# Two projections of the first network with three groups side by side, and weighted values between two input tiles

## The reference

```
g = sigmoid(gate_logit).reshape(b, s, 3, d)
merged = (g[:, :, 0] * (y_fox @ w_o_fox[l])
          + g[:, :, 1] * (y_mla @ w_o_mla[l])
          + g[:, :, 2] * (y_sb @ w_o_sb[l]))
x = x + gt_a * (merged @ w_out[l])
u = rms_norm(x, g_ffn[l]) * (1 + sc_f) + sh_f
```

## Time and profile before

| what | value |
|---|---|
| median of 3 runs | 2102.11 us (2101.72 to 2104.12) |
| the profiled execution | 2101.66 us, its span 2099.9 us |
| TensorE busy | 2025.5 us (96%) |
| VectorE busy | 1624.7 us (77%) |
| ScalarE busy | 1171.1 us (56%) |
| mean granted TensorE clock | 0.992 |
| end of the attention, layer 0 | 264 to 306 us of the span |
| end of the attention, layer 1 | 738 to 779 us of the span |

### The profile page before, as it was taken

One profiled execution on the slowest core, in us unless ns is written; L12 is line 12 of the kernel. 1 busy time (PEld: TensorE's weight loads), 2 busy tenths in 40 slices (PEclk: granted clock), 3 DMA queues, 4 the chain that ended last, 5 costly groups with the idle time before them and its releaser, 6 DMA issues.

```text
span 2099.9 us, 37052 instructions
## 1 busy us (share of the span) xinstructions
PE 2025.5 (96%) x13975; PEld 1837.7 (88%) x13975; DVE 1624.7 (77%) x2668; ACT 1171.1 (56%) x2116; POOL 148.3 (7%) x233
## 2 busy tenths in 40 slices
PE   6999989999999989999999999999999999999998
PEld 6988989999988989998876888888888888899997
DVE  7788879966688879979787789786989426658983
ACT  6757746645557756646636555352544227646762
POOL 0100000000000000004000300001102000000000
PEclk9999999999999999999999999999999999999999
DMA  9766547865766547876341334546634222244553
GB/s 367 272 216 203 189 146 258 282 229 167 241 216 210 180 153 258 300 243 219 126 162 62 107 131 156 194 141 240 211 130 142 99 90 101 81 161 141 184 178 110
DMA packets 106624, 383.03 MB, mean 182 GB/s; under 512 B 11504, under 2 KB 16128, under 8 KB 105184
## 3 DMA queue, kind: packets, MB, share of 16 engines
q1 hardware_dynamic: 77584, 280.21, 39.2%
q0 software_dynamic: 25792, 94.31, 13.4%
q10 hardware_dynamic: 3088, 6.29, 0.8%
HBM read 379.71 MB, written 1.05 MB: 181 GB/s over the span
## 4 chain that ended last, share of the span: by engine, by line
PE 77%; DVE 12%; ACT 4%; issue 4%; DMA 3%; POOL 0%; POOLq 0%; SPq 0%; DVEq 0%; ACTq 0%
PE ps L1099 19%; PE ps L1102 18%; PE ps L1103 18%; DVE ring_l L2379 3%; PE ps L1120 3%; PE ps L1124 3%; PE ps L1125 3%; DVE ada_junk L2402 2%; DMA work<-adas_in 2%; PE ps L1142 2%; ACT ring_r L1722 2%; PE ps L1145 1%; PE ps L1146 1%; PE ps L1672 1%; DMA ring<-tape_in 1%
## 5 line engine op out<-in xcount | busy, mean ns | idle before, releaser
L1099 PE MATMUL ps<-part,ring_l 128*128 128x256 f32 (+1 forms) x3445 | 1038.6, 301 | 13.7 <-DVE ring_l L2379 7.3
L1103 PE MATMUL ps<-part,ring_r 128*128 128x256 f32 (+1 forms) x3445 | 1027.2, 298 | 0.0
L1102 PE MATMUL ps<-part,ring_r 128*128 128x256 f32 (+1 forms) x3445 | 1026.1, 298 | 0.0
L2379 DVE TENSOR_TENSOR ring_l<-ring,ring_r 128x1024 fp32r<-128x1024 f32 x514 | 626.4, 1232 | 149.5 <-ACT ring_r L1722 146.8
L1722 ACT ACTIVATE ring_r<-ring 128x1024 fp32r<-128x1024 f32 x514 | 533.8, 1056 | 356.8 <-DMA ring<-tape_in 259.1
L1099 PEld LDWEIGHTS ps<-part,ring_l 128*128 128x128 f32 x3445 | 652.0, 189 | 44.2 <-DVE part L2379 7.7
L1103 PEld LDWEIGHTS ps<-part,ring_r 128*128 128x128 f32 x3445 | 648.6, 188 | 24.7
L1102 PEld LDWEIGHTS ps<-part,ring_r 128*128 128x128 f32 x3445 | 648.5, 188 | 24.3
L2402 DVE SCALAR_TENSOR_TENSOR ada_junk<-work 128x1024 bf16<-128x1024 f32 x272 | 334.0, 1228 | 50.2 <-DMA work<-adas_in 38.2
L1142 PE MATMUL ps<-part,ring_l 128*128 128x256 f32 (+1 forms) x400 | 125.5, 314 | 20.9 <-DVE part L2379 11.1
L1146 PE MATMUL ps<-part,ring_r 128*128 128x256 f32 (+1 forms) x400 | 121.5, 304 | 0.0
(11 more groups left out here) (287 smaller groups left out, 2109.0 us busy)
## 6 DMA issues: line engine op xcount, KB each, us to landing
ring<-tape_in SPq DMA_DIRECT2D x514, 512.0 KB, 3.4
work<-adas_in POOLq DMA_DIRECT2D x176, 512.0 KB, 4.7
work<-ada_first_in SPq DMA_DIRECT2D x8, 1024.0 KB, 17.5
work<-bias_in ACTq DMA_DIRECT2D x1, 2048.0 KB, 7.9
x<-x_t_in SPq DMA_DIRECT2D x1, 1024.0 KB, 7.5
work<-cond_in POOLq DMA_DIRECT2D x1, 1024.0 KB, 8.9
x<-ctx_in ACTq DMA_DIRECT2D x1, 1024.0 KB, 13.1
x<-dist_in ACTq DMA_DIRECT2D x1, 1024.0 KB, 6.2
```

The lines of the kernel that those rows point to most:

```text
L1099: mm = pe.matmul(dst, lhsT=wl, rhs=mr, start=(k == 0), stop=False)
L1102: pe.matmul(dst, lhsT=wr, rhs=mr, start=False, stop=False)
L1103: mm = pe.matmul(dst, lhsT=wr, rhs=ml, start=False, stop=(k == len(moving) - 1))
L2379: return dve.tensor_tensor(dst, whole, rounded_part.bitcast(F32), ALU.subtract)
```

## The change

- The third branch's first three groups run side by side (input tile by input tile, with a wait for each y), and pv11 is issued inside them, behind input tile 1 (`VALUES_LATE`). Before, pv11 stood ahead of the branch. The other five groups run one after the other as before.
- w_out's first three groups run side by side; the others as before.
- The host reorders the tape's tiles to match.
- ScalarE rounds by hand where `READ` no longer has a name: `round_behind` after the last mix tile, and one panel more behind each of the first three squares.
- VectorE's `ahead` for w_out0, 1 and 2 uses leads of 6, 7 and 8, since the three groups now start in the same panel.

```diff
+VALUES_LATE = 1
...
     for b, n in enumerate(("w_o_fox", "w_o_mla", "w_o_sb")):
-        out += [gate[ends[b] * KD:ends[b + 1] * KD], stationary(i[n][l])]
-    out += [stationary(i["w_out"][l])]
+        o = stationary(i[n][l])
+        if b == N_BRANCH - 1:
+            o = np.concatenate([abreast(*(o[f * WT:(f + 1) * WT] for f in range(ABREAST))), o[ABREAST * WT:]])
+        out += [gate[ends[b] * KD:ends[b + 1] * KD], o]
+    w_out = stationary(i["w_out"][l])
+    out += [abreast(*(w_out[f * KD:(f + 1) * KD] for f in range(ABREAST))), w_out[ABREAST * KD:]]
...
-                    if p - 1 > STICKS:
+                    if PAIRS >= p > STICKS + 1:
                         weighted_values(p - 2)
                     b = branch_at(p)
-                    if b is not None:
+                    if b == N_BRANCH - 1:
+                        project_abreast([f"branch{b}_{f}" for f in range(ABREAST)], pairs(y_r, y_l, WT),
+                                        lambda k: y_made((N_BRANCH - 1) * PER_BRANCH + k, l),
+                                        lambda k: weighted_values(PAIRS - 1) if k == VALUES_LATE else None)
+                        for f in range(ABREAST, KD):
+                            project(f"branch{b}_{f}", pairs(y_r, y_l, WT))
+                    elif b is not None:
...
-                for f in range(KD):
-                    project(f"w_out{f}", pairs(mix_r, mix_l, KD), (lambda k: mix_made(k, l)) if f == 0 else None)
+                project_abreast([f"w_out{f}" for f in range(ABREAST)], pairs(mix_r, mix_l, KD), lambda k: mix_made(k, l))
+                for f in range(ABREAST, KD):
+                    project(f"w_out{f}", pairs(mix_r, mix_l, KD))
...
                 round_mix(KD - 1)
+                round_behind(READ[f"branch{N_BRANCH - 1}_{KD - 1}"])
                 for k in range(KD):
                     act.wait_ge(*x_mixed(k, l))
                     act.activation(sq[:, k, :], xt[:, k, :], ACT.Square).then_inc(squared.sem, 1)
+                    if k < ABREAST:
+                        round_panels(READ[f"branch{N_BRANCH - 1}_{KD - 1}"] + RING + k + 1)
...
-                    ahead(f"w_out{f}", l, AHEAD if f < KD - 1 else AHEAD - 2)
+                    ahead(f"w_out{f}", l, AHEAD + f if f < ABREAST else AHEAD if f < KD - 1 else AHEAD - 2)
```

More of the change, by code:

```diff
@@ L1222, in project, with project_abreast @@
                     READ[name] = tile_at[0] // TILES_PER_PANEL
-                def project_abreast(names, moving, ready):
-                    for mm in linear_abreast([open_bank(n)[:, 0:T] for n in names], moving, ready):
+                def project_abreast(names, moving, ready, beside=None):
+                    for mm in linear_abreast([open_bank(n)[:, 0:T] for n in names], moving, ready, beside):
                         mm.then_inc(group_done.sem, 1)
```

## The result

The changed kernel takes 2089.99 us (median of 7 runs, 2082.49 to 2091.14), the kernel before 2101.72 us in the runs beside it. The ratio is 0.9942, 95% interval 0.9926 to 0.9957: faster by 0.6%, or 11.7 us between the medians. The forecast was 2092.2 us, between 2089.0 and 2097.0.

A forecast was written before the change was run, and what follows sets the result against it. TensorE, busy 96% of the span, was the bound, so only its idle or slow stretches could give time. Layer 0 (5.9 or 4.8 us) plus layer 1 (5.1 or 4.0), middle 9.9: 2102.1 - 9.9 = 2092.2 us, range 2089.0 to 2097.0.

The forecast's parts named there:

- The waits around pv11 and the branch: Third branch, layer 0: 18 matmuls go ahead of pv11, which starts at 266.81; TensorE then idles only about 0.1 us.
- The mix parts in time: w_out's inputs from VectorE: chain of about 12.5 us, last mix part at 282.6 to 282.8; cost 0 to 0.2 us.
- The tightest tile: w_out's input tile with least slack for its mix part: tile 5, needed at 282.0 and made at about 282.0.
- w_out's end: VectorE's and ScalarE's x-update loop stays hidden; stat matmul 1.28 us after the last matmul; cost 0, layer 1 gains 0.76.
- the count: Step-by-step times of x updates after the three groups end: x0 at -0.6 us, x6 at +12.3; x7 waits for TensorE.
- the loop does not catch up: Rival at w_out's end: late roundings, six intervals of 3.06 us, 4.7 us lost a layer; 2101.6 us, chance 0.06.
- the clock cost 1.6 us: w_out, layer 0: some 16 matmul steps at 0.213 instead of 0.113 us behind the mix_l waits.
- the rule weighed: Clock throttling follows a free-running window, so the 1.6 us may return behind another gap: 8.3 us gained, not 9.9.
- the first rival: Clock falls at another gap, or w_out's mix tiles 5 to 7 wait: 2093.8 to 2096.7 us, chance 0.18.
- The sum: Gain up to the stat matmul: layer 0 5.9 or 4.8 us, layer 1 5.1 or 4.0; middle 9.9.
- The slower rival: Mix chain delayed by ScalarE's ring DMA waits, last mix part at 291.3: 3.8 us slower, up to 2107; chance 0.03.
- the faster one: Feed-forward stages flip to the fast matmul pace, 5.5 us in layer 0, the same in layer 1: 2086.7 or 2081; chance 0.05.

The follow-up runs named there:

- branch alone: The kernel before with only the third branch and the weighted values changed, w_out left as before; ratio 0.9988 (0.9974 to 1.0002).

## Why the prediction was right

**The waits around pv11 and the branch.** Right: pv11 0.14 us from the forecast, and no wait behind it. y was even there before TensorE wanted it, because the 2.19 us from pv11 to y held a rounding on ScalarE that no longer stands in between (1.81 us without it).

**The mix parts in time.** Right in the main, with the chain at 13.0 us instead of about 12.5, started 0.35 sooner. The tightest tile was the wrong one: tile 5 was named, and the gap of 0.23 us stands ahead of tile 4, in each of the three stretches at the fast pace. It is a little over the 0.2 us that the prediction allowed to any wait for mix_l.

**w_out's end.** Right: the distances of the x updates followed the count within 0.2 us up to x6, and the loop went off the path. The rival "the loop does not catch up" fell: even without the leads it costs about 1.1 us a layer and not 4.7. Its step that failed is the one that let each of x0 to x6 take 3.06 us; only updates with a rounding and a split between them do.

**The clock.** The step "the clock cost 1.6 us" was mis-sized: the slow steps are there, but the stretch got only 0.86 us longer, since VectorE's and ScalarE's loop stood 0.8 us behind TensorE. The sum does not use this term, since it goes from row to row; the rule weighed (8.3 us instead of 9.9) and the first rival do, and they put the clock too high. That it can move was right: with the waits of layer 0 filled, the clock fell in layer 1 behind another gap. The Trainium skill (TensorE: Matmul & The Clock Gate, Part 1) lets the point of change hang on a free-running window. The two layers of these traces agree, 0.52 in one and steps of 0.113 us in the other behind like waits; that the fall stands at the same place in both executions of the kernel before is not explained by it. In the changed kernel no fall stands in either stretch. Outside them the clock does fall, in the kernel before too and at places that change from one execution to the next (0.97 from 1540 to 1600 us in the second execution of the kernel before, 1.00 in the first), so that no fall there can be laid to the change.

**The sum.** 8.8 to 11.0 us were forecast for the stretches; 10.3 were measured in the first profile, with layer 0 at the slow and layer 1 at the fast pace, and 10.8 in the second (38.27 twice, against the first profile of the kernel before). Some of the closeness is luck. At the fast pace 38.2 us were forecast for layer 0's stretch and 38.27 came, but tile 3 was reached 0.27 us sooner than forecast and the part from there to w_out's end took 0.38 us longer, so that the early y and the gap ahead of tile 4 nearly cancel. At the slow pace there is no gap, and 38.83 came for 39.3. The rest of the 11.7 between the medians is not the change's own: it lies in code that both programs share. One piece alone is larger: over 1100 steps from 1900.12 on took 131.2 us at the slow pace in the first profile of the kernel before, and the same piece took 126.6 at the fast pace in its second profile and in both of the changed kernel. The executions of one program differ by more than the 1.3 us: the kernel before took between 2090.0 and 2109.6 us in 27 runs beside one set of experiments.

**The slower rival and the faster one.** The last mix part was made at 282.76, 7 us sooner than the 290 from which the slower rival decides. The feed-forward stage of layer 0 took the fast pace for its first 73 us (305.03 to 378.26), where it was slow before. It is worth some 1.5 us (from 309.99 to 459.57 before, from 305.03 to 453.13 after) and not the 2.8 of its 646 steps, since short gaps open behind it, such as one of 0.19 us for a panel's rest at 384.43.

## What to carry to other kernels

Where the first group of a projection waits for inputs that arrive one by one, run a few groups side by side, input tile by input tile: the wait turns into work. How many can be read from the trace: enough that the inputs are there when they are wanted, and few enough that the engines which read the results have groups left to hide behind (here three; two cost 1.7 us a layer, four gained nothing). Before a slow clock or a wait is priced, look at what stands right behind it, and compare versions by the stretch that the edit touches when the whole span wanders by more than the edit is worth.

## What was not expected of the hardware

The same matmul shape runs at one of two paces at full granted clock, 0.1134 or 0.1178 us, and keeps it over hundreds of instructions (1117 steps in a row at the fast one in the changed kernel from 1894.41 on, 1270 at the slow one in the kernel before from 309.99 on). Two executions of one program differed by 6.3 us, all of it behind the first network. Which pace a stretch takes was not found. A wait can end in either: behind the last wait for mix_l in layer 1 the pace was 0.1178 in branch alone and 0.1134 in the kernel before.

Behind two waits of 1.4 and 0.5 us with three matmuls between them the granted clock fell to 1.2 GHz in both profiles of the kernel before, in layer 0 and not in layer 1. Behind waits of 0.95 and 1.22 us around the eight matmuls of pv11 it fell once, in one of the eight stretches (four profiles) that have such waits. Branch alone had 0.48, 1.65 and 0.50 us and kept its clock.
